# Taking the convolution's matmuls of layer 0 in steps inside its attention

## The chip, the cores and the metric

The kernel runs on one core of one Trainium2 chip. The metric is the device time of one execution in microseconds; before the change the median of three runs is 2084.97 us (2084.91 to 2086.41).

## The reference

Two blocks run on one sequence of 256 tokens of width 1024 (with 256 context tokens beside it in the first block). The change lies in layer 0 of the first block, cut here to what matters:

```python
def even_mixer(h_lat, h_ctx, w_in, conv_w, q_g, k_g, rpb, w_out, need_ctx):
    def query_side(p):
        gb, gc, u, q = jnp.split(p, [CONV_CH, 2 * CONV_CH, 3 * CONV_CH], -1)
        y_conv = gb * dwconv3(gc * u, conv_w)
        return y_conv, rms_norm(split_heads(q, NA_HEADS), q_g)
    ...
    p_lat = h_lat @ w_in
    ...
    y_na = merge_heads(neighbourhood_attention(q_lat, k_lat, v_lat, k_ctx, v_ctx, rpb))
    y_lat = jnp.concatenate([yc_lat, y_na], -1) @ w_out
```

The same is done for the context tokens (dense attention instead of the neighbourhood one). `gb`, `gc` and `u` are 512 columns each of one product with `w_in`; 8 heads of 64 attend over 512 keys (latent tokens) or 256 (context tokens). Beside it the layer's modulation vectors are products of silu(c), silu(c_ctx) with `ada_w`. A feed-forward stage, a second layer (two attentions, mixture of experts) and a second block follow.

## The kernel before

**Products.** Every fp32 product is made of three matmuls on high and low halves of both operands (`mm3`, L825 to L827: low x high, high x low, high x high). A weight tile (1 MB, 128 x 2048 in SBUF) is sent for by SyncE (`load_tiles`, L2741), its high half rounded by ScalarE (L1261), its low half subtracted by VectorE (L1754). Tiles stand in one list, `TILES`, in the order in which TensorE uses them (`use`). A tile gets the least recently used open slot; `t.prev` is the tile that had the slot before. SyncE sends for tiles strictly in list order, each when `t.prev` is done.

**Look-ahead.** ScalarE and VectorE call `feed(events)` ahead of each wait. `place[event]` is the number of tiles that TensorE's program has taken when it signals the event; with `n` the largest of these, `next_tiles` (L562) hands out tiles of the list, in order, up to `n + 2`, and stops at the first that may not be handed out:

```python
if t.gate != at["gate"] or t.slot not in at["slots"] or i >= n + at["sums" if t.sums else "ahead"] or (t.prev is not None and t.prev > n - 2):
    return
```

**Sum tiles.** A modulation product of 256 rows is done by VectorE alone (`summed`, L1760): four multiplications with a running sum (L1770) of raw tile and `CB`, the rows of silu(c), which ScalarE makes (L1420). Such tiles stand in the same list and slots (`sums`). For VectorE `at["sums"]` is 0 until layer 0's attention is over, so a sum tile i needs i < n; ScalarE (2) only passes over them. In the attention `pump(2)` does up to two of the four multiplications a step.

**Layer 0.** TensorE computes q, v and k (`proj`, two tiles each, four token tiles of 128), turning q by transpositions before k's product. The keys are normed by ScalarE (squares, L1385), VectorE (L1871, L1808, L1875) and GpSimd (L2640), turned (`head_turn`; VectorE L2059, ScalarE L1306, VectorE L1803). Then six convolution tiles (`feat`: c, u, g for channels 0 and 1, then for 2 and 3; two features of 128 channels a tile, 8 x 3 matmuls of 512 columns a feature), with the k transpositions behind the second tile. GpSimd masks the two bias tables (L2673) after the k norms. VectorE takes c x u, three taps, times g (L2093 to L2109).

**Attention** (`attend`, L908, L1308, L1960) runs 32 units, token tile by token tile, 8 heads each; the first 16 have 512 keys and a bias added by TensorE (L927), the other 16 have 256 keys. Step i gives TensorE: scores of unit i, transpositions (L831) of unit i-3, P·V (L948) of unit i-4, and after each token tile four more transpositions of its output. VectorE takes the maximum (L1978, L1984), ScalarE the exponential (L1318); they copy transposed probabilities in turns (L2009, L1326). Scores and transpositions share a ring of five PSUM banks. Twelve sum tiles (parts 2, 3, 4) stand at steps 1 + n*9//4, the gate rows of part 2 at step 16. The output projection (`proj` "o") follows.

Of the kernel before, what the change touches and what calls it, by code (L numbers as in the profile page):

```python
# [14 lines left out]
ALU = mybir.AluOpType  # L15
# [182 lines left out]
class Weight:  # L198
# [20 lines left out]

    def t(self):  # L220
        return Weight(self.name, None, self.at, True)
# [4 lines left out]
    def of(self, arrays):  # L226
        x = arrays[self.name][tuple(slice(*p) if isinstance(p, tuple) else p for p in self.at)]
        x = x.T if self.turned else x
        k, n = x.shape[0] // 128, x.shape[1]
        return x.reshape(k, 128, n).transpose(1, 0, 2).reshape(-1)  # L230


class Packed:
# [5 lines left out]
    def place(self, w):  # L239
        key = w.key()  # L240
        if key not in self.start:
            n = 1
            for p in w.at:
                n *= p[1] - p[0] if isinstance(p, tuple) else 1
# [23 lines left out]
def _build(nc, ctx, I, cst_d, scr_d, out_d, packed):  # L268
# [64 lines left out]
    XSa = Region("xs", LA.col).some(2, 1024)  # L333
    YC = v3(LA.pair(2048), 4)
# [7 lines left out]
    RP = CUB[:, 0:128]  # L342
    assert LA.col <= CB0
    XQ = [XSa[i // 2][:, (i % 2) * 512:(i % 2 + 1) * 512] for i in range(4)]
    slot_e = [slot(WORK + n) for n in (0, 4096, 14336, 18432, 22528)]
    LB = Region("att", LB0)
    YNT = v3(LB.pair(2048), 4)
    Pa = LB.some(4, 512)
    PTa = LB.some(2, 512)
    YNa = LB.some(2, 512)  # L350
    TMPa = LB.some(4, 512)
# [210 lines left out]
    def next_tiles(at, *events):  # L562
        n = max([place[event] for event in events], default=0)
        while at["tile"] < len(TILES):
            i, t = at["tile"], TILES[at["tile"]]
            if t.gate != at["gate"] or t.slot not in at["slots"] or i >= n + at["sums" if t.sums else "ahead"] or (t.prev is not None and t.prev > n - 2):
# [40 lines left out]
    class Heads:  # L607

        def __init__(self, units, lag, p, pt, fin):
            self.units, self.lag, self.p, self.pt, self.fin = units, lag, p, pt, fin  # L610
            self.slot_of, self.held, self.sums, self.gates = {}, {}, {}, {}
# [20 lines left out]
    HEADS = {}  # L632

# [89 lines left out]
    def mla_units():  # L723
# [13 lines left out]
        "a0": dict(fresh=[("clo", 3)], masks=[], out_free=[("clo", 3)]),  # L737
# [17 lines left out]
    CONV = ((512, "c"), (1024, "u"), (0, "g"))  # L755
# [3 lines left out]
    def tensor_program(e):  # L759
        due = Due(book)  # L760
        state = dict(tile=0, due=due, gate="", sums=iter(()))
# [21 lines left out]
        def sums(p, jj):  # L783
# [13 lines left out]
        def gate_rows(p):  # L797
            n = 8 * MODS[p][3]
            b = take("m", "gt", p)
# [4 lines left out]
        def consumed(t, *event):  # L804
            t.done = event
            for p, jj in itertools.islice(state["sums"], 1):
# [3 lines left out]
                 "m": (5,), "y": (4, 5, 6, 7)}  # L810
# [58 lines left out]

        def mod_product(p, hf, kh, ring="m"):  # L870
# [37 lines left out]
        def attend(st):  # L908
            A = HEADS[st]
            for i in A.steps():  # L910
                for p, jj in A.sums.get(i, ()):
                    sums(p, jj)
                if A.has(i):
# [3 lines left out]
                    for x, (q, keys) in enumerate(u.qk):  # L917
                        b = take("5", "score", st, i, x)
# [10 lines left out]
                        m.then_inc(*done("score", st, i, x))  # L929
                j = i - A.lag  # L930
                if A.has(j):
                    b = take("5", "turn", st, j)
# [19 lines left out]
                if A.has(j) and A.units[j].last:  # L952
                    g = A.units[j].group
                    y, nc_ = A.fin[g][:2]
                    b = take("5", "fin", st, g)
# [5 lines left out]
                if i in A.gates:  # L961
                    gate_rows(A.gates[i])
# [29 lines left out]
        for jj in range(2):  # L992
            for c0, nm in CONV:
                feat(("conv", nm, jj), AT4a, w_ev[:, c0:c0 + 512], 2 * jj, 2, 512, normed("a", 0) + normed("a", 1), "8")
                if jj == 0 and nm == "u":
                    for t in range(4):
                        head_turn(("k", t), XQ[t], 4, [("hn", "k", t)], "o")
        attend("a0")
# [10 lines left out]
        state["sums"] = iter([(p, jj) for p in (5, 6, 7, 8, 9, 10, 11) for jj in range(4)])  # L1009
# [239 lines left out]
    def scalar_program(e):  # L1249
# [58 lines left out]
        def attend(st):  # L1308
            A = HEADS[st]
            for i in A.steps():  # L1310
                if A.has(i):
# [1511 lines left out]
```

## Time and profile before

| | |
|---|---|
| median of three runs | 2084.97 us |
| the profiled execution, its span | 2084.66 us, 2082.8 us |
| PE busy | 1829.2 us (88%), 8622 matmuls |
| DVE, ACT, POOL busy | 1256.2, 819.2, 120.6 us |
| mean granted clock of TensorE | 0.874 of full |

PE is TensorE's matmuls, PEld its weight loads, DVE VectorE, ACT ScalarE, POOL GpSimd, SP SyncE. An idle time in brackets at a row's end stands before the instruction and names what ended it. A clock of 1.00 is 2.4 GHz, 0.50 is 1.2 GHz. Matmul ends are modelled, so the distance between starts is what to read.

### The profile page before, as it was taken

How to read it: one execution, taken by the hardware profiler on the slowest of the kernel's cores; microseconds unless marked ns; L12 is line 12 of the kernel's file. 1: busy time of each engine (PE TensorE's matmuls, PEld its weight loads, DVE VectorE, ACT ScalarE, POOL GpSimd, SP SyncE). 2: the span in 40 equal slices, each digit the busy share in tenths (PEclk: the TensorE clock that was granted, in tenths of full speed). 3: DMA queues.
4: the chain of work that ended last, by engine and by line, in shares of the span. 5: the costliest groups of instructions: out<-in, count | busy, mean ns of one | idle time of the engine just before them, and what ended most of it. 6: DMA issues, size and time to landing. Idle time of an engine off the chain costs nothing. (4 is left out here: it accounts for less than half of the span.)

```text
span 2082.8 us, 21348 instructions
## 1 busy us (share of the span) xinstructions
PE 1829.2 (88%) x8622; PEld 1526.9 (73%) x8622; DVE 1256.2 (60%) x1716; ACT 819.2 (39%) x993; POOL 120.6 (6%) x116
## 2 busy tenths in 40 slices
PE   4999997699999995969867999999968988878997
PEld 2787776578778884748646888888858866767986
DVE  5365674368665534544636988888866545555643
ACT  5322222322213314212314777777744432435532
POOL 1130000200020011220010000000000000000000
PEclk8899556799999997975676999999989985998999
DMA  6422241235555522210033888888844520125552
GB/s 277 118 91 91 81 142 61 81 130 194 213 197 188 195 77 72 101 61 21 1 146 112 324 327 324 329 323 330 330 176 162 194 97 1 61 82 193 182 201 101
DMA packets 61145, 332.54 MB, mean 160 GB/s; under 512 B 16803, under 2 KB 17378, under 8 KB 27889
## 3 DMA queue, kind: packets, MB, share of 16 engines
q1 hardware_dynamic: 55792, 321.54, 42.5%
q10 hardware_dynamic: 4354, 6.32, 1.0%
q0 software_dynamic: 896, 3.26, 0.4%
q8 instruction: 70, 1.15, 0.2%
q14 instruction: 33, 0.27, 0.0%
HBM read 329.96 MB, written 1.13 MB: 159 GB/s over the span
## 5 line engine op out<-in xcount | busy, mean ns | idle before, releaser
L1754 DVE TENSOR_TENSOR wlo__69<-raw__68,whi__70 128x2048 fp32r<-128x2048 f32 (+2 forms) x67 | 148.0, 2209 | 80.3 <-ACT whi__70 L1261 80.1
L1261 ACT ACTIVATE whi__70<-raw__68 128x2048 fp32r<-128x2048 f32 (+2 forms) x67 | 120.0, 1791 | 146.8 <-DMA raw__68<-in_ffn_w 69.6
L1754 DVE TENSOR_TENSOR wlo__61<-raw__60,whi__62 128x2048 fp32r<-128x2048 f32 (+4 forms) x54 | 121.1, 2243 | 92.2 <-ACT whi__62 L1261 92.2
L1754 DVE TENSOR_TENSOR wlo__65<-raw__64,whi__66 128x2048 fp32r<-128x2048 f32 (+4 forms) x54 | 104.0, 1927 | 55.9 <-ACT whi__66 L1261 55.8
L1261 ACT ACTIVATE whi__62<-raw__60 128x2048 fp32r<-128x2048 f32 (+4 forms) x54 | 98.1, 1816 | 82.6 <-DMA raw__60<-in_ev_w_in 30.5
L2640 POOL TENSOR_TENSOR keep__58<-keep__58,keep__59 128x1 f32<-128x1 f32 (+3 forms) x48 | 45.4, 946 | 1212.5 <-DVE keep__58 L1808 1212.5
L1261 ACT ACTIVATE whi__66<-raw__64 128x2048 fp32r<-128x2048 f32 (+4 forms) x54 | 87.4, 1619 | 62.0 <-DMA raw__64<-in_od_w_in 19.2
L1978 DVE TENSOR_REDUCE keep__58<-ps 128x1 f32<-128x256 f32 (+1 forms) x104 | 56.6, 544 | 40.9 <-PE ps L827 34.1
L1261 ACT ACTIVATE whi__145<-raw__143 128x2048 fp32r<-128x2048 f32 (+2 forms) x16 | 28.1, 1754 | 131.3 <-DMA raw__143<-in_ffn_w 131.3
L825 PE MATMUL ps<-ffn__124,wlo__144 128*128 128x512 f32 x176 | 69.8, 397 | 8.2 <-DVE wlo__144 L1754 7.0
L1754 DVE TENSOR_TENSOR wlo__144<-raw__143,whi__145 128x2048 fp32r<-128x2048 f32 (+2 forms) x16 | 33.5, 2091 | 64.7 <-ACT whi__145 L1261 64.7
L826 PE MATMUL ps<-ffn__125,whi__145 128*128 128x512 f32 x176 | 69.5, 395 | 0.0
L827 PE MATMUL ps<-ffn__124,whi__145 128*128 128x512 f32 x176 | 69.5, 395 | 0.0
L1770 DVE SCALAR_TENSOR_TENSOR wsum__67<-raw__64,silu_rows 128x1024 f32<-128x1024 f32 x56 | 68.6, 1252 | 0.5
L1770 DVE SCALAR_TENSOR_TENSOR wsum__63<-raw__60,silu_rows 128x1024 f32<-128x1024 f32 x56 | 68.6, 1252 | 0.5
L825 PE MATMUL ps<-ffn__124,wlo__69 128*128 128x512 f32 x168 | 66.1, 394 | 2.7 <-issue 2.7
L827 PE MATMUL ps<-ffn__124,whi__70 128*128 128x512 f32 x168 | 66.1, 394 | 0.0
L826 PE MATMUL ps<-ffn__125,whi__70 128*128 128x512 f32 x168 | 66.0, 393 | 0.0
L1754 DVE TENSOR_TENSOR wlo__222<-raw__221,whi__223 128x2048 fp32r<-128x2048 f32 x24 | 54.9, 2288 | 4.1 <-ACT whi__223 L1261 4.1
L1754 DVE TENSOR_TENSOR wlo__226<-raw__225,whi__227 128x2048 fp32r<-128x2048 f32 x24 | 54.9, 2288 | 0.0
L1754 DVE TENSOR_TENSOR wlo__230<-raw__229,whi__231 128x2048 fp32r<-128x2048 f32 (+1 forms) x24 | 50.7, 2112 | 3.8 <-ACT whi__231 L1261 3.8
L1261 ACT ACTIVATE whi__223<-raw__221 128x2048 fp32r<-128x2048 f32 x24 | 45.8, 1910 | 5.7 <-DMA raw__221<-in_moe_w 5.7
(1082 smaller groups left out, 5432.4 us busy)
## 6 DMA issues: line engine op xcount, KB each, us to landing
raw__221<-in_moe_w SPq DMA_DIRECT2D x24, 1024.0 KB, 6.2
raw__225<-in_moe_w SPq DMA_DIRECT2D x24, 1024.0 KB, 6.3
raw__60<-in_ada_w SPq DMA_DIRECT2D x19, 1024.0 KB, 6.9
raw__64<-in_ada_w SPq DMA_DIRECT2D x19, 1024.0 KB, 7.0
raw__229<-in_moe_w SPq DMA_DIRECT2D x16, 1024.0 KB, 5.7
raw__68<-in_moe_w SPq DMA_DIRECT2D x16, 1024.0 KB, 6.0
raw__60<-in_moe_w SPq DMA_DIRECT2D x16, 1024.0 KB, 6.8
raw__68<-in_ffn_w SPq DMA_DIRECT2D x14, 1024.0 KB, 4.9
```

Of the source, the lines that this page charges most:

```text
L825: e.matmul(out, ll, rh, start=start, stop=False)
L826: e.matmul(out, lh, rl, start=False, stop=False)
L827: return e.matmul(out, lh, rh, start=False, stop=stop)
L1261: e.activation(t.hi(), t.raw(), ACT.Copy).then_inc(*did("hi", i))
L1754: e.tensor_tensor(t.lo(), t.raw(), t.hi().bitcast(F32), ALU.subtract).then_inc(*did("lo", i))
L1770: m = e.scalar_tensor_tensor(out=junk, in0=slot_raw[t.slot][:, c * 1024:c * 1024 + 1024], scalar=1.0, in1=CB[:, v * D:(v + 1) * D], op0=AL ...
L1978: e.tensor_reduce(neg, b[:, 0:u.total], AX.X, ALU.max).then_inc(*link())
L2640: e.tensor_tensor(x, x, EXPO[:, 0:1].broadcast_to([128, n_]) if n_ > 1 else EXPO[:, 0:1], ALU.pow).then_inc(*did(out, *key))
```

## The change

The convolution's products are written as a generator, `convolved`, that yields after each step of three matmuls (96 steps, 8 a feature). Sixteen steps (features c0, u0) are taken before the first k transposition, the other 80 inside the attention, between the scores of unit i and the transpositions of unit i-3: `FILLED` gives 16 + (i+1)*80//28 steps taken after step i, so that step 27 takes the last. Features now go channel by channel (c, u, g), and a weight tile holds two features whose columns aren't adjacent (`Weight.columns`, laid side by side in the packed weights). VectorE's and ScalarE's parts of the convolution are called from `attend` one step after a feature is complete (`CONV_AT`), the final rounding of its output at steps 28 to 32.

Around it: the attention's ring has four banks, the convolution's two (4 and 5). Buffers move: the convolution's output `YC` takes the place of the normed input after it is last read, the probabilities lie in the q/k staging, the attention's output in the place of q. Two of the twelve sum tiles now stand in k's product, the other ten at steps 0, 3, ... 27; from k's product to the end of the attention, weight tiles use slots 0 and 1 and sum tiles slot 2. The gate rows come at step 12. silu(c) is made before k's squares. A sum's multiplications are taken one at each `feed`, or all when the tile after next is reached. `next_tiles` gets a stricter condition for the slot's last tile.

```diff
+        busy = max([i for i in range(max(n - 4, 0), n) if not TILES[i].sums], default=0)
         while at["tile"] < len(TILES):
             i, t = at["tile"], TILES[at["tile"]]
-            if t.gate != at["gate"] or ... or (t.prev is not None and t.prev > n - 2):
+            if t.gate != at["gate"] or ... or (t.prev is not None and t.prev >= min(n - 1, busy)):
                 return
...
-    for n, (p, jj) in enumerate((p, jj) for p in (2, 3, 4) for jj in range(4)):
-        HEADS["a0"].sums[1 + n * 9 // 4] = [(p, jj)]
-    HEADS["a0"].gates = {16: 2}
+    for n, (p, jj) in enumerate(SUMS[2:12]):
+        HEADS["a0"].sums[n * 3] = [(p, jj)]
+    HEADS["a0"].gates = {12: 2}
+    HEADS["a0"].ring = "4"
...
+    CONV = dict(c=512, u=1024, g=0)
+    FEATS = [(nm, j) for j in range(4) for nm in "cug"]
+    FILLED = [16 + (i + 1) * 80 // 28 if i < 27 else 96 for i in range(40)]
+    CONV_AT = {f: min(i for i in range(-1, 40) if ([16] + FILLED)[i + 1] >= 8 * (n + 1)) for n, f in enumerate(FEATS)}
...
-                s = min(open_slots, key=lambda s: last_in.get(s, s - 100))
+                s = min(state["loads"] or open_slots, key=lambda s: last_in.get(s, s - 100))
...
-                s = min(open_slots, key=lambda s: last_in.get(s, s - 100))
+                s = min(state["adds"] or open_slots, key=lambda s: last_in.get(s, s - 100))
...
+        def convolved():
+
+            w = W["ev_w_in"][0]
+            for f in range(0, 12, 2):
+                two = [(CONV[nm] + j * 128, CONV[nm] + j * 128 + 128) for nm, j in FEATS[f:f + 2]]
+                tile, hi, lo = use(w.columns(*two), KT, 256)
+                for i, key in enumerate(FEATS[f:f + 2]):
+                    b = take("c", "conv", *key)
+                    for k in range(KT):
...
+                        m = mm3(b, sub((hi, lo), slice(None), k, slice(i * 128, i * 128 + 128)),
+                                sub(AT4a, slice(None), k), k == 0, k == KT - 1)
...
+                        yield
...
                         m.then_inc(*done("score", st, i, x))
+                advance(fill, FILLED[i] - (FILLED[i - 1] if i else 16))
                 j = i - A.lag
...
+        state.update(sums=iter(SUMS[0:2]), loads=(0, 1), adds=(2,))
         proj(("l0", "k"), x4(AT4a), 4, KT, w_ev[:, 2048:2560], 512, rdy("a"))
...
+        state["sums"] = iter(())
+        for t in range(4):
+            if t == 0:
+                fill = convolved()
+                advance(fill, 16)
+            head_turn(("k", t), XQ[t], 4, [("hn", "k", t)], "o")
+        attend("a0", fill)
+        state.update(loads=None, adds=None)
```

VectorE's look-ahead and its part of the convolution:

```diff
         def feed(*events):
+            n = max([place[event] for event in events], default=0)
+            pump(9 if at["sum"] <= n - 2 else 1)
             for i, t in next_tiles(at, *events):
                 if t.sums:
                     pump(9)
-                    at["begun"] = summed(i, t)
-                    if at["sums"]:
+                    at["begun"], at["sum"] = summed(i, t), i
+                    if i <= n - 2:
                         pump(9)
                     continue
...
+        def convolved(i):
+            for j in range(4):
+                g, cv = GC[:, (j % 2) * 512:(j % 2 + 1) * 512], CV0[j]
+                if i == CONV_AT["u", j] + 1:
...
+                    feed(("prod", "conv", "u", j))
...
+                if i == CONV_AT["g", j] + 1:
+                    feed(("prod", "conv", "g", j))
...
+                if i == CONV_AT["g", 3] + 2 + j:
+                    feed(("prod", "conv", "g", 3))
+                    low("clo", (j,), YC[1][:, j, :], cv, YC[0][:, j, :], ("chi", j))
+        attend("a0", convolved)
         pump(9)
         at["sums"] = 2
```

## Rows read from the trace of the kernel before

**Rows 1.** Page, part 2: the clock granted to TensorE, 40 slices

```profile
PEclk8899556799999997975676999999989985998999
```

**Rows 2.** Windows: length, busy PE PEld DVE ACT POOL, clock, DMA share, GB/s

```profile
131.60:203.90 72.30, 68.99 (x305) 56.53 (x303) 41.41 (x44) 14.52 (x16) 16.82 (x6) 0.98 0.26 88
203.90:347.00 143.10, 124.26 (x484) 99.49 (x484) 96.67 (x195) 37.01 (x89) 1.14 (x2) 0.53 0.30 103
```

**Rows 3.** Windows, 10 us each, in the attentions a2 and a3

```profile
1720.00:1730.00 10.00, 10.00 (x34) 6.93 (x33) 4.69 (x15) 2.80 (x10) 0.00 (x0) 0.50 0.01 2
1800.00:1810.00 10.00, 9.21 (x61) 7.54 (x60) 5.67 (x20) 5.60 (x20) 0.00 (x0) 1.00 0.01 2
```

**Rows 4.** Timeline of PE, layer-0 attention: start, length, line, tiles, count

```profile
236.23 0.58 PE L825 MATMUL ps<-in__75,in__74 64*128 64x256 f32 x1
...
238.31 0.58 PE L825 MATMUL ps<-in__75,in__74 64*128 64x256 f32 x1
...
239.25 1.11 PE L831 MATMUL ps<-keep__49,att__113 128*128 128x128 f32 x4
240.16 1.81 PE L948 MATMUL ps<-in__77,att__116 128*128 128x64 f32 x8
241.89 0.58 PE L825 MATMUL ps<-in__75,in__74 64*128 64x256 f32 x1
```

**Rows 5.** Timeline of PE, the first steps of that attention

```profile
209.34 0.66 PE L831 MATMUL ps<-keep__49,att__112 128*128 128x128 f32 x4
209.93 0.38 PE L825 MATMUL ps<-in__75,in__74 64*128 64x256 f32 x1
...
211.10 0.38 PE L825 MATMUL ps<-in__75,in__74 64*128 64x256 f32 x1
...
211.65 0.66 PE L831 MATMUL ps<-keep__49,att__113 128*128 128x128 f32 x4
```

**Rows 6.** Timelines of SP and of ACT: weight tiles sent for and rounded

```profile
120.68 0.33 SPq L2741 DMA_DIRECT2D raw__64<-in_ev_w_in  x1
131.56 0.33 SPq L2741 DMA_DIRECT2D raw__68<-in_ev_w_in  x1
...
125.58 1.92 ACT L1261 ACTIVATE whi__66<-raw__64 128x2048 fp32r<-128x2048 f32 x1 [7.72 <-DMA raw__64<-in_ev_w_in]
```

**Rows 7.** Timeline of PE: last k transposes, start of output projection

```profile
158.14 0.66 PE L831 MATMUL ps<-keep__49,xs__79 128*128 128x128 f32 x4 [1.39 <-DVE xs__78 L2059]
158.55 0.56 PE L825 MATMUL ps<-in__84,wlo__69 128*128 128x512 f32 x1
...
162.28 0.39 PE L825 MATMUL ps<-in__84,wlo__69 128*128 128x512 f32 x1
...
346.27 0.78 PE L825 MATMUL ps<-whi__62,in__81 128*128 128x512 f32 x1
```

**Rows 8.** Timeline of DVE, from the q tiles to the convolution

```profile
116.08 0.69 DVE L1803 TENSOR_TENSOR in__74<-xs__79,in__73 128x512 fp32r<-128x512 f32 x1 [0.70 <-ACT in__73 L1306]
...
127.53 2.29 DVE L1754 TENSOR_TENSOR wlo__65<-raw__64,whi__66 128x2048 fp32r<-128x2048 f32 x1 [7.34 <-ACT whi__66 L1261]
129.74 0.68 DVE L1871 TENSOR_REDUCE keep__58<-in__86 128x8 f32<-128x512 f32 x1
...
142.69 6.07 DVE L1754 TENSOR_TENSOR wlo__69<-raw__68,whi__70 128x2048 fp32r<-128x2048 f32 x1
...
155.30 0.74 DVE L2059 TENSOR_SCALAR xs__78<-ps,keep__51 128x512 f32<-128x512 f32 x1
...
163.50 0.68 DVE L2093 TENSOR_TENSOR in__89<-in__88,ps 128x512 f32<-128x512 f32 x1
```

**Rows 9.** Timeline of POOL: the second bias table's mask

```profile
146.57 6.65 POOL L2673 TENSOR_TENSOR in__83<-in__83,keep__49 128x2048 f32<-128x2048 f32 x1
```

**Rows 10.** Timeline of DVE: two of a sum tile's four multiplications

```profile
207.83 1.23 DVE L1770 SCALAR_TENSOR_TENSOR wsum__63<-raw__60,silu_rows 128x1024 f32<-128x1024 f32 x1
...
208.98 1.22 DVE L1770 SCALAR_TENSOR_TENSOR wsum__63<-raw__60,silu_rows 128x1024 f32<-128x1024 f32 x1
```

More of the change, by code:

```diff
@@ L226, in of @@
     def of(self, arrays):
-        x = arrays[self.name][tuple(slice(*p) if isinstance(p, tuple) else p for p in self.at)]
+        x = arrays[self.name]
+        if isinstance(self.at[-1][0], tuple):
+            x = np.concatenate([x[..., slice(*span)] for span in self.at[-1]], -1)
+        at = [p for p in self.at if not (isinstance(p, tuple) and isinstance(p[0], tuple))]
+        x = x[tuple(slice(*p) if isinstance(p, tuple) else p for p in at)]
         x = x.T if self.turned else x
@@ L342, in _build @@
     RP = CUB[:, 0:128]
+    PTa = LA.some(2, 512)
     assert LA.col <= CB0
@@ L345, in _build @@
     slot_e = [slot(WORK + n) for n in (0, 4096, 14336, 18432, 22528)]
+    YNT, Pa = QT3, XQ
+    YNa = [BREV[0][:, t * 512:(t + 1) * 512] for t in range(2)]
     LB = Region("att", LB0)
[L347 to L351, printed above, removed]
+    YC, TMPa = v3(LB.pair(2048), 4), LB.some(4, 512)
     LF = Region("ffn", WORK)
@@ L563, in next_tiles @@
         n = max([place[event] for event in events], default=0)
+        busy = max([i for i in range(max(n - 4, 0), n) if not TILES[i].sums], default=0)
         while at["tile"] < len(TILES):
             i, t = at["tile"], TILES[at["tile"]]
-            if t.gate != at["gate"] or t.slot not in at["slots"] or i >= n + at["sums" if t.sums else "ahead"] or (t.prev is not None and t.prev > n - 2):
+            if t.gate != at["gate"] or t.slot not in at["slots"] or i >= n + at["sums" if t.sums else "ahead"] or (t.prev is not None and t.prev >= min(n - 1, busy)):
                 return
@@ L632, in _build @@
     HEADS = {}
+    SUMS = [(p, jj) for p in range(2, 12) for jj in range(4)]
     def prob(st, i):
@@ L760, in tensor_program @@
         due = Due(book)
-        state = dict(tile=0, due=due, gate="", sums=iter(()))
+        state = dict(tile=0, due=due, gate="", sums=iter(()), loads=None, adds=None)
         open_slots, turn_of = [0, 1, 2] + slot_e, Counter()
@@ L795, in sums, with gate_rows @@
                 last_in[s] = i
-        def gate_rows(p):
+        def gate_rows(p, ring="m"):
             n = 8 * MODS[p][3]
-            b = take("m", "gt", p)
+            b = take(ring, "gt", p)
             for s, n_ in state["due"](("gsum", p)):
@@ L917, in attend @@
                     for x, (q, keys) in enumerate(u.qk):
-                        b = take("5", "score", st, i, x)
+                        b = take(A.ring, "score", st, i, x)
                         at = 0
@@ L954, in attend @@
                     y, nc_ = A.fin[g][:2]
-                    b = take("5", "fin", st, g)
+                    b = take(A.ring, "fin", st, g)
                     for s, n in state["due"](("fy", st, g)):
@@ L1008, in tensor_program @@
             lent[slot_f] = [("prod", "o", 0, 1, 3), ("res", ("o", 0), 1, 3)]
-        state["sums"] = iter([(p, jj) for p in (5, 6, 7, 8, 9, 10, 11) for jj in range(4)])
+        state["sums"] = iter(SUMS[12:])
         nf = normed("f", 0) + normed("f", 1)
@@ L1731, in vector_program @@
     def vector_program(e):
-        at = dict(tile=0, due=Due(book), gate="", chain=0, ahead=2, sums=0, slots={0, 1, 2, *slot_e}, begun=None)
+        at = dict(tile=0, due=Due(book), gate="", chain=0, ahead=2, sums=0, slots={0, 1, 2, *slot_e}, begun=None, sum=0)
         def due(*events):
```

140 lines of the change are left out of this document (67 added, 73 removed).

## The prediction

> **What bounds the kernel now.** I read the page's clock line first, then the stages, then single steps. TensorE is the busiest engine, and its clock is granted at about half for three slices, 220 to 350 us [rows 1]. The windows say what that is: from 131.6 to 203.9 us the convolution's products run at 0.98, from 203.9 to 347 the attention of layer 0 runs at 0.53 with TensorE busy for 124 of 143 us [rows 2]. It is not the dependence on softmax that sets this stage but TensorE at 1.2 GHz; VectorE is busy for 96.7 us of it. The clock is no fixed property of attention: the later attention a2 stood at 0.50 while never idle, a3 at 1.00 with gaps in it [rows 3].
>
> One wide step (units 0 to 15) at half clock repeats every 5.66 us (236.23 to 241.89): scores 3.02, transpositions 0.91, the P·V products 1.73; one block of 256 keys is 0.94 of it [rows 4]. At 2.4 GHz the same pieces took 1.72 (209.93 to 211.65), 0.59 and 0.55 for the block [rows 5]. No P·V of this stage ran at full clock, so I take half of 1.73, 0.87 (an estimate). A step of the convolution is three matmuls of 512 columns. A tile of 48 of them is 10.9 us at full clock (120.68 to 131.56, when SP could reuse its slot) [rows 6], 0.227 each, 0.68 a step. After the short waits of the k turns nine of them took 3.73 (158.55 to 162.28), 0.41 each, 1.24 a step, until the clock was back: 1.7 us lost [rows 7]. The output projection starts at 346.3 [rows 7]. VectorE writes a tile's low half in 2.29 us; the k norms take 13.0 (129.74 to 142.7), the k turns 8.2 (155.30 to 163.50); between them two low halves took 12.6 instead of 5.3 [rows 8], while POOL masked the bias tables, until 153.2 [rows 9].
>
> **The change, step by step.** The work of TensorE stays: 96 convolution steps, 32 units. 16 steps now stand ahead of the k transpositions and 80 go 2 to 3 at a time between score i and transposition i-3. If nothing waited and the clock stayed up, the interleaved stage would cost 16 x (1.72+0.59+0.87) = 50.9, 16 light units x (0.55+0.30+0.44) = 20.6, four output turns 2.4, and 80 x 0.68 = 54.4: 128.3 us [rows 5, 6]. That is the gain. Against it stand waits that come from the order in which halves are prepared. The low half of a tile is written by VectorE in list order, a sum tile (a modulation product) can't begin before TensorE's program has passed it, and what lies behind it in the list waits too.
>
> *k's second tile.* A sum tile now stands ahead of it in the list. VectorE is free at 116.8 [rows 8], but its rows of silu(c) are computed on ScalarE only after the last q rounding, about 1.9 us like a copy of the same size [rows 6]: 118.0. Four multiplications 1.15 apart [rows 10] end at 122.7, the low half at 125.0. TensorE wants it at 120.7, where tile one was given back [rows 6]. 4.3 us idle, 1.7 for the clock: k ends at 137.6, not 131.6.
>
> *The first convolution tile.* Its transfer stands on SP's queue behind that of the second sum tile, which waits for the first sum (122.7). One load takes 4.9 us [rows 6]; I take 7.8 for the second of two (an estimate, 7 to 9). ScalarE waits for it ahead of k's squares, rounds until 132.4, squares until 133.0; the norms end 13.0 later, at 146.0. Then come the second sum, 4.6, and the low half, 2.3: 152.9. The bias masks start on POOL at the same point of its program as before, so I add the 7.3 us that the collision cost [rows 8, 9]: 160.2 (bounds 152.9 and 160.2; I take the upper since the two subtracts were hit alike). TensorE stands for 22.6 us. The 16 steps, 10.9 + 1.7, end at 172.8. The k turns' chain, 0.6 + 8.2, has no products beneath it any more: scores begin at 181.6, 22 us ahead of before, with 80 steps still to do.
>
> By the Trainium skill (SBUF — State Buffer, Who interferes with whom) a VectorE instruction with two SBUF inputs contends with a GpSimd instruction that reads SBUF, so the sum's multiplications should be slowed like the subtracts. By that rule the 160.2 stands; were sums exempt, it would be 156.5. The rows show only the subtracts.
>
> *Start of the attention.* VectorE first does the first channel's taps (four operations of 0.5 to 0.75, 2.7) and a low half (2.3), against 3.0 of scores: 2 us. The clock is down after the wait: 3. ScalarE's look-ahead holds an exponential while a sum is finished: 1. Together 6.
>
> *Three waits inside.* The sum tiles at steps 9, 15 and 21 reuse slot 2 straight after another sum tile. The new condition in the look-ahead lets such a tile through only for an event counted after a later product tile; that product tile, the next of the convolution, stands behind it. So at steps 11, 17 and 22 TensorE asks for a tile whose halves VectorE writes only after this step's maximum (0.85 wide, 0.6 narrow), the whole sum (4.6) and its subtract (2.3): 7.8 less one convolution step 0.7 is 7.1; 7.5; and 7.5 less 1.4 plus about 2 for a late transfer, 8. Behind the waiting matmul are queued the step's transpositions and P·V. 22.6 us in all. A stand of this length before had the clock down, so each costs half-clock time besides: 1.7 as in that row's stretch [rows 7] if the products were dense, up to 6 as they are mixed; I take 3, 9 in all.
>
> *The end.* The draining steps have nothing beneath them: 4. The last sum tile (step 27) is let through only after the attention, ahead of the output projection's first low half: final rounding and subtract 1.7, 4.6, 2.3 = 8.6. Before, that half lay ready.
>
> *At nothing:* the ring of four PSUM banks (a score needs the exponential of two steps before, 0.85 + 0.9 us against steps of 5.1; if that cover goes it is one of the waits above); the two convolution banks (given back one feature, 2.8 steps, earlier); moved buffers; gate rows at step 12 on PE, VectorE and POOL, needed over 100 us later; VectorE's load, at most 96.7 + 41.4 us [rows 2] in 179. Sums in the feed-forward stage are begun in one look-ahead and finished in the next: same work, 0, bounds -4 and +4.
>
> **Sum:** 181.6 + 128.3 + 6 + 22.6 + 9 + 4 + 8.6 = 360.1 us for the output projection's start, against 346.3: +13.8. The profiled execution took 2084.66 us (span 2082.8), 0.3 below the median of 2084.97: 2098.5 from the one, 2098.8 from the other; I say 2098. The bounds of the steps (collision 0, clock 1.7 to 6 each, transfer, feed-forward) give this case 2084 to 2118.
>
> **The rivals.**
> *The halves come in time inside the attention* (faster). Place: steps 11, 17, 22 and the projection's start. If the sum is done early there, 22.6 + 9 + 6.9 = 38.5 go: 2060. It decides from 14 us on, so gaining little more than a third of it is enough. If the two waits ahead of the attention go as well (4.3 + 1.7 + 22.6 + 1.7 = 30.3), 2030. For it: VectorE has some 40 us of slack in the stage, and transfers are early. Against it: the order is a static list, and slack can't be used by what isn't let through.
>
> *The clock stays at half* (much slower). At 1.2 GHz the stage is 16 x 5.66 + 16 x 2.26 + 3.6 = 130.4 [rows 4] plus 80 x 1.24 = 99.2 [rows 7]: 229.6 instead of 128.3, less the 12 already allowed: +89, 2187; each tenth of the stage at half clock is 10 us. For it: 80 us of that attention never lifted it, and every long wait drops it. Against it: the clock came back within 3.9 us of 512-column products [rows 7], and a3 kept 1.00 with small matmuls.
>
> The Trainium skill (Perfetto Trace Analysis, Matmul Optimizations) says that the matmul engine scales its power with utilization and that matmuls should be executed back to back in batches, which speaks against cutting twelve batches into pieces. By that rule the time is this rival's; the trace shows the clock going either way in attentions [rows 3].
>
> **How the numbers follow.** Forecast 0.50; halves in time 0.28; in between (some of the waits, 2075 to 2089) 0.10; clock at half for much of the stage 0.12. Within 0.2% (4 us, about what a measurement of this kernel can tell from no change) lie most of the in-between case and the forecast's edge: 0.10. Faster 0.31, slower 0.59. The range leaves out the full rival of 2030 (0.07) and most of the half-clock case (0.09): 2052 to 2130. The likeliest case's own range is 2084 to 2118.
>
> **What would show it.** TensorE's first convolution matmul near 160 us, waiting for VectorE; three waits of 6 to 9 us of a first-term matmul (now in the convolution) for a low half, each behind four sum multiplications; one of 7 to 9 at the output projection; clock near 1.00 between them. Wrong if low halves of convolution tiles are written before the sum preceding them or more than a step ahead of use, if the clock reads 0.5 through the interleaved steps, or if the feed-forward stage moves by over 4 us.

## The result and the profile after

The changed kernel is slower: 2119.76 us (median of four executions, 2112.61 to 2128.69) against 2084.94 (2083.86 to 2086.41), a ratio of 1.0169, 95% interval 1.0122 to 1.0215. The forecast was 2098, range 2052 to 2130: right in direction and inside the range, 22 us short, and just outside the likeliest case's own range (2084 to 2118). The profiled execution took 2125.05 us (span 2123.2, mean clock 0.880), 5.3 above its median. The four times stand in two pairs, 2112.61 and 2114.46, 2125.05 and 2128.69, with the median between them where no execution lies; the profiled one is of the slower pair. That matters below.

The page of the kernel after: busy tenths of TensorE and granted clock in 40 slices of 53 us, to hold against [rows 1].

```profile
PE   4958887869899996887975999999986989787997
PEclk8976897979999998895675999999998985898999
```

The slices of half clock of before (5, 5, 6) are gone. From the fourth to the eighth slice stand 6 to 9, and TensorE's busy time has fallen to 1813.5 us of 2123.2, from 1829.2 of 2082.8: much of its time at half clock was exchanged for time in which it stands. Where it stands, from k's second tile to the output projection (rows of PE: start, duration, line and operation, and in brackets the idle time before it and what ended it; in this kernel L839 is the first matmul of a triple, L845 a transposition):

```profile
124.76 0.77 PE L839 MATMUL ps<-whi__62,in__87 128*128 128x512 f32 x1 [4.46 <-DVE wlo__61 L1797]
160.26 0.76 PE L839 MATMUL ps<-in__86,wlo__65 128*128 128x512 f32 x1 [21.53 <-issue]
...
182.48 0.55 PE L839 MATMUL ps<-in__75,in__74 64*128 64x256 f32 x1 [4.88 <-ACT in__75 L1346]
187.38 0.76 PE L839 MATMUL ps<-in__86,wlo__61 128*128 128x512 f32 x1 [1.83 <-issue]
258.60 0.77 PE L839 MATMUL ps<-in__86,wlo__61 128*128 128x512 f32 x1 [7.02 <-issue]
298.44 0.77 PE L839 MATMUL ps<-in__86,wlo__65 128*128 128x512 f32 x1 [8.79 <-issue]
326.95 0.77 PE L839 MATMUL ps<-in__86,wlo__61 128*128 128x512 f32 x1 [6.77 <-issue]
...
374.83 0.76 PE L839 MATMUL ps<-whi__66,att__115 128*128 128x512 f32 x1 [8.83 <-DVE wlo__65 L1797]
```

These are the waits of the prediction, one by one: k's second tile (forecast 4.3, at 125.0), the first convolution tile (forecast at 160.2), the scores (181.6), three inside the attention (7.1, 7.5, 8: 22.6; measured 22.58), the projection (8.6). In five of the rows the bracket says only "issue"; the row's second operand, `wlo`, is a low half, and VectorE's rows ahead of the matmul at 258.60 show who wrote it and after what:

```profile
250.72 0.69 DVE L2025 TENSOR_REDUCE keep__58<-ps 128x1 f32<-128x512 f32 x1 [4.39 <-PE ps L841]
251.44 0.15 DVE L2031 TENSOR_SCALAR keep__58<-keep__58 128x1 f32<-128x1 f32 x1
251.51 1.22 DVE L1813 SCALAR_TENSOR_TENSOR wsum__71<-raw__68,silu_rows 128x1024 f32<-128x1024 f32 x1
...
255.07 1.22 DVE L1813 SCALAR_TENSOR_TENSOR wsum__71<-raw__68,silu_rows 128x1024 f32<-128x1024 f32 x1
...
256.21 2.29 DVE L1797 TENSOR_TENSOR wlo__61<-raw__60,whi__62 128x2048 fp32r<-128x2048 f32 x1
```

The maximum, four multiplications of the sum, the subtract. Just ahead VectorE had stood for 4.39 us: it had the time, but the list didn't let it have the tile. ScalarE is held by the same list: the tile was sent for at 237.30, and its high half was rounded only from 252.31.

The balance of the two profiled executions (spans 2082.8 and 2123.2, +40.4), from the starts of the same events: output projection's first matmul 346.27 and 374.83, +28.6 (forecast +13.8); last gating behind the projection 391.82 and 421.07, +0.7 more; last gating of the feed-forward stage 792.83 and 829.20, +7.1 more (forecast 0, bounds -4 and +4; a second profile of the same kernel, after_again below, gives +5.1); first gating behind the second layer's attention 1065.76 and 1105.31, +3.2 more; the rest +0.9.

### The profile page after: what moved, and what is told of

Same layout as the page of the kernel before. It is cut to its first block and busy times, and to the rows that moved or that the text cites. A ratio compares the mean times of both kernels' runs of the same rounds, so it can differ in the third digit from the quotient of the medians.

```text
span 2123.2 us, 21351 instructions
## 1 busy us (share of the span) xinstructions
PE 1813.5 (85%) x8622; PEld 1508.2 (71%) x8622; DVE 1255.3 (59%) x1716; ACT 819.4 (39%) x993; POOL 122.2 (6%) x116
## 5 line engine op out<-in xcount | busy, mean ns | idle before, releaser
L1797 DVE TENSOR_TENSOR wlo__69<-raw__68,whi__70 128x2048 fp32r<-128x2048 f32 (+3 forms) x64 | 136.2, 2129 | 71.9 <-ACT whi__70 L1301 71.9
L1301 ACT ACTIVATE whi__70<-raw__68 128x2048 fp32r<-128x2048 f32 (+3 forms) x64 | 114.2, 1785 | 141.0 <-DMA raw__68<-in_ffn_w 66.4
L1301 ACT ACTIVATE whi__62<-raw__60 128x2048 fp32r<-128x2048 f32 (+4 forms) x56 | 91.3, 1630 | 102.8 <-DMA raw__60<-in_ev_w_in 47.7
L1301 ACT ACTIVATE whi__66<-raw__64 128x2048 fp32r<-128x2048 f32 (+4 forms) x55 | 100.0, 1817 | 67.4 <-DMA raw__64<-in_ev_w_in 21.8
L1301 ACT ACTIVATE whi__141<-raw__139 128x2048 fp32r<-128x2048 f32 (+2 forms) x16 | 28.1, 1754 | 141.6 <-DMA raw__139<-in_ffn_w 141.6
L1797 DVE TENSOR_TENSOR wlo__140<-raw__139,whi__141 128x2048 fp32r<-128x2048 f32 (+2 forms) x16 | 33.5, 2092 | 79.4 <-ACT whi__141 L1301 79.4
L839 PE MATMUL ps<-ffn__120,wlo__140 128*128 128x512 f32 x176 | 69.9, 397 | 8.3 <-DVE wlo__140 L1797 7.2
L839 PE MATMUL ps<-ffn__120,wlo__69 128*128 128x512 f32 x168 | 65.5, 390 | 2.7 <-issue 2.7
L1813 DVE SCALAR_TENSOR_TENSOR wsum__71<-raw__68,silu_rows 128x1024 f32<-128x1024 f32 x48 | 65.3, 1385 | 2.2 <-ACT silu_rows L1445 1.2
L1813 DVE SCALAR_TENSOR_TENSOR wsum__67<-raw__64,silu_rows 128x1024 f32<-128x1024 f32 x40 | 50.4, 1283 | 0.5
L1813 DVE SCALAR_TENSOR_TENSOR wsum__63<-raw__60,silu_rows 128x1024 f32<-128x1024 f32 x40 | 49.4, 1257 | 0.5
```

Source lines behind the costliest of these rows:

```text
L839: e.matmul(out, ll, rh, start=start, stop=False)
L1301: e.activation(t.hi(), t.raw(), ACT.Copy).then_inc(*did("hi", i))
L1797: e.tensor_tensor(t.lo(), t.raw(), t.hi().bitcast(F32), ALU.subtract).then_inc(*did("lo", i))
L1813: m = e.scalar_tensor_tensor(out=junk, in0=slot_raw[t.slot][:, c * 1024:c * 1024 + 1024], scalar=1.0, in1=CB[:, v * D:(v + 1) * D], op0=AL ...
```

## Experiments

The theory: each wait comes from the order in which tiles are let through, at the place where the prediction put it; the clock's loss behind the waits adds to it. The rivals: the clock is held down by the mixture of matmuls itself, or VectorE has no slack. Times of the kernel before, measured beside each group: 2083.14 us (13 executions) beside the first four runs, 2083.87 (7) beside the best three, 2082.91 (7) beside `first_step` and `after_again`, 2082.33 (13) beside the last. All code below is cut; "..." marks what is left out.

### two_slots: two buffers for the sums

```diff
...
+        if book.counting:
+            last_in.update({s: last_in[2] for s in slot_h})
+            state["adds"] = slot_h
         attend("a0", fill)
...
```

> Inside the attention the sum tiles get two raw buffers (the two halves of slot 2) in turn, so that no sum tile reuses the buffer of the tile just before it and none is held back by the look-ahead; nothing else is changed. Theory A (the waits come from the order in which halves are let through, and the clock falls because of them): the three waits of 7.0, 8.8 and 6.8 us at a convolution matmul and the 8.8 us at the output projection go, 31.4 us, and with them up to 8 us of half clock between 250 and 370 us. The projection starts at 335 to 344 instead of 374.8 and the time is 2080 to 2089 instead of 2119.8. Theory B (the mixed stage itself holds the clock down): the waits go, but the clock reads 0.5 to 0.8 in their place, projection not before 355, time 2100 or more. Theory C (VectorE has no slack): the waits come back as waits of scores for the maxima, time 2110 or more.

Measured: 2092.39 us (10 executions, 2085.12 to 2101.03), 1.0053 of before [1.0035, 1.0071]; 27 us less than the changed kernel's 2119.76, 3 us above what theory A gave. (The two buffers are the halves of slot 2; the products' unused output goes to one idle buffer, so each multiplication also waits for the one before it.) All three waits inside and the one at the projection are gone from the rows, and the projection starts at 349.99 instead of 374.83. But 24.8 us came, not 31 to 40: other waits took part of their place. Its rows of PE with more than 1.5 us of idle time between 190 and 350 us:

```profile
294.09 1.71 PE L997 MATMUL ps<-in__77,in__93 128*128 128x64 f32 x8 [3.29 <-ACT in__93 L1384]
...
335.33 1.12 PE L997 MATMUL ps<-in__77,in__93 128*128 128x64 f32 x4 [4.50 <-ACT in__93 L1384]
...
349.99 0.76 PE L850 MATMUL ps<-whi__66,att__118 128*128 128x512 f32 x1 [1.56 <-issue]
```

P·V (L997) waits for ScalarE's copy of the transposed probabilities. At 294 ScalarE had been held in its look-ahead by a late transfer, with an exponential and that copy queued behind:

```profile
291.19 1.91 ACT L1317 ACTIVATE whi__62<-raw__60 128x2048 fp32r<-128x2048 f32 x1 [7.72 <-DMA raw__60<-in_ev_w_in]
```

That transfer was sent for at 282.74, behind a sum's on SP's queue (282.37), which had to wait for its buffer until the sum before it was done. At 335 it was VectorE, with two multiplications and the closing product of a convolution channel (330.79 to 333.80) ahead of a maximum in the light steps. So theory A holds for the waits; B doesn't from 220 to 290 us, where the clock reads 1.00; C holds for one wait of 4.5 us. What this run leaves as it was is the half clock at the attention's start: 0.50 until 212 us here too.

### late_sums: and no sum in k's product

```diff
...
-    for n, (p, jj) in enumerate(SUMS[2:12]):
-        HEADS["a0"].sums[n * 3] = [(p, jj)]
-    HEADS["a0"].gates = {12: 2}
+    for i, (p, jj) in zip((1, 3, 6, 9, 12, 15, 18, 20, 23, 25), SUMS[0:10]):
+        HEADS["a0"].sums[i] = [(p, jj)]
+    HEADS["a0"].gates = {14: 2}
...
-        state.update(sums=iter(SUMS[0:2]), loads=(0, 1), adds=(2,))
+        state.update(loads=(0, 1))
...
+        state.update(loads=None, adds=None, sums=iter(SUMS[10:12]))
...
```

> The same two buffers, and no sum tile in k's product: ten sums stand at steps 1 to 25 of the attention, never more than two between two convolution tiles, the last two in the output projection. Theory A: k's second tile is not waited for (4.5 us), the first convolution matmul starts near 133 us instead of 160.3, the scores at 155 to 160 instead of 182.5, and the clock, which read 0.50 from 180 to 210 us after the long wait, is back within some 5 us: projection start 300 to 315, time 2045 to 2062. Theory B (the half clock at the attention's start belongs to the mixed stage and not to the wait before it): again 25 to 30 us at 0.50 behind the first scores, time 2060 to 2075. Theory C: VectorE, with more in fewer us, makes the scores wait; time 2075 or more.

Measured: 2065.31 us (4 executions, 2058.97 to 2069.06), 0.9916 [0.9886, 0.9945]: 3 us above theory A's range and within B's in time, with its projection at 310.89 as A had it. The clock tells the two apart. Its rows of PE at the k turns, the first scores and the projection:

```profile
149.22 1.12 PE L856 MATMUL ps<-keep__49,in__79 128*128 128x128 f32 x4 [4.23 <-DVE in__78 L2122]
154.12 1.12 PE L856 MATMUL ps<-keep__49,in__79 128*128 128x128 f32 x4 [3.79 <-DVE in__78 L2122]
159.66 0.55 PE L850 MATMUL ps<-in__75,in__74 64*128 64x256 f32 x1 [4.42 <-ACT in__75 L1362]
...
310.89 0.76 PE L850 MATMUL ps<-whi__66,att__118 128*128 128x512 f32 x1 [1.56 <-issue]
```

The clock was back some 5.9 us behind the first scores (0.50 until 165 us, 1.00 from 166), not 25 to 30 as B had it, and it read 1.00 from 170 to 280: with the same steps mixed in, the stage holds full clock for 110 us on end. What differs from the changed kernel is the waits.

### ffn_finish: the feed-forward stage's old rule

```diff
-                    if i <= n - 2:
+                    if at["sums"] or i <= n - 2:
                         pump(9)
```

> Only the rule of the feed-forward stage is put back: a sum begun there is finished in the same look-ahead. If this rule made the new wait of 4.7 us at 579.6 us and the rest of the 7 us by which the stage became longer, the distance from the output projection's last gating to the last one of the feed-forward stage falls from 408 to about 401 us and the time by 7 us, to 2113. If the stage is longer for another reason (tiles that arrive later, the clock), nothing moves.

Measured: 2112.49 us (2110.05, 2114.93). Two executions say nothing of a gain, as five of the changed kernel's eight (below) are about as fast; the distance within the profile does. From the projection's last gating to the stage's last: 400.7 us (417.70 to 818.42), 408.1 in the changed kernel (406.1 in after_again), 401.0 before. All of the 5 to 7 us are this line's. How it works, in the changed kernel (PE's wait, the subtract it waited for, and SP's two issues before it; L2786 sends for a tile):

```profile
579.55 0.77 PE L839 MATMUL ps<-whi__141,ffn__128 128*128 128x512 f32 x1 [4.66 <-DVE wlo__140 L1797]
...
577.12 2.29 DVE L1797 TENSOR_TENSOR wlo__140<-raw__139,whi__141 128x2048 fp32r<-128x2048 f32 x1 [3.46 <-ACT whi__141 L1301]
...
567.85 0.33 SPq L2786 DMA_DIRECT2D raw__64<-in_ada_w  x1
568.22 0.43 SPq L2786 DMA_DIRECT2D raw__139<-in_ffn_w  x1
```

and in ffn_finish, the same two transfers and the same matmul:

```profile
558.04 0.43 SPq L2786 DMA_DIRECT2D raw__64<-in_ada_w  x1
563.11 0.33 SPq L2786 DMA_DIRECT2D raw__139<-in_ffn_w  x1
...
572.91 0.47 PE L839 MATMUL ps<-whi__141,ffn__128 128*128 128x512 f32 x1 [1.36 <-DVE wlo__140 L1797]
```

The two kernels stand 3.3 us apart here (the product tile sent for before these, into raw 139, at 550.10 and 546.79); the rest of each distance is the edit's. A sum begun in one look-ahead and finished in the next moves the moment at which its slot (raw 64) is free: it is sent for at 567.85 instead of 558.04, 6.5 us later beyond the 3.3. SP sends in list order, so the product tile behind it (raw 139) starts 1.8 us late, and it now travels beside the sum's tile: ScalarE has it 6.95 us after its sending (568.22 to 575.17) instead of 5.13 (563.11 to 568.24). Both together make the wait longer, 4.66 us instead of 1.36. I had put the spreading at "same work, 0"; the work was the same, the moment at which the buffer came free was not.

One more thing is seen here by accident. Ahead of the feed-forward stage this is the changed kernel, and yet its projection starts at 371.36, not at 374.83; first_step and after_again below take this up.

### masks_early: the bias masks ahead of the k norms

```diff
...
         for w in ("q", "k"):
+            if w == "k":
+                for t in range(2):
...
+                    for s, n in due(("brev",), ("cst",), ("lo", place["prod", "l0", "k", 3] - 1)):
...
```

> GpSimd masks the bias tables ahead of the k norms (once k's second low half is written, about 125 us) instead of behind them. If the collision made the second sum cost 12.8 instead of 4.6 us, its four multiplications take about 1.2 us each, the k norms end some 1.5 us later because GpSimd is busy until 135, and the first convolution matmul starts at 153 to 154.5 instead of 160.3; time 2112 to 2115. If the multiplications were slow for another reason they stay at 4.9 and 5.5 us and the start at 160 to 162.

Measured: 2111.99 us (2109.52, 2114.47; again two, hardly below the changed kernel's faster five, so the rows decide), first convolution matmul at 152.98 (expected 153 to 154.5) instead of 160.26. The second sum of the changed kernel, while GpSimd masked (144.52 to 154.45):

```profile
145.20 4.90 DVE L1813 SCALAR_TENSOR_TENSOR wsum__71<-raw__68,silu_rows 128x1024 f32<-128x1024 f32 x1
...
150.03 5.50 DVE L1813 SCALAR_TENSOR_TENSOR wsum__71<-raw__68,silu_rows 128x1024 f32<-128x1024 f32 x1
...
155.57 1.22 DVE L1813 SCALAR_TENSOR_TENSOR wsum__71<-raw__68,silu_rows 128x1024 f32<-128x1024 f32 x1
```

and of this kernel, with GpSimd masking from 124.65 to 133.78:

```profile
145.90 1.22 DVE L1813 SCALAR_TENSOR_TENSOR wsum__71<-raw__68,silu_rows 128x1024 f32<-128x1024 f32 x1
```

So a multiplication with two SBUF inputs took four times as long beside GpSimd's addition; the two together were 8.0 us longer, and the first convolution matmul moved by 7.3. The Trainium skill (SBUF — State Buffer, Who interferes with whom) says that a VectorE instruction with two SBUF inputs contends with a GpSimd instruction that reads SBUF, which the prediction had weighed; the trace agrees, 4.90 and 5.50 against 1.22 us.

### best: all three edits together

> late_sums with both other edits: sums of the feed-forward stage finished where they are begun, and the bias masks made on GpSimd as soon as VectorE has written the last turned q. Theory A (the losses are single waits with places of their own, and add): the k turns lose the waits of 4.2, 3.8 and 4.4 us at 149 to 160 us, which stand over low halves and turns slowed by the masks, so the scores start at 151 to 154 instead of 159.7 (-7), and the feed-forward stage gives 6 to 7: 2065.3 - 13 to 14 = 2051, range 2046 to 2056. Theory B (the parts share one slack): only the feed-forward part shows, 2058 to 2060.

Its masks wait for `("qlo", "q", 3)` instead. Measured: 2055.28 us (4 executions, 2054.45 to 2056.20), 0.9864 [0.9848, 0.9881]: faster than before by 28.6 us. The feed-forward stage gave its 6.4 (400.25 us against 406.67 in late_sums). The masks gave 3.1, not 7: scores start at 156.58. Rows of PE and, last, of DVE:

```profile
124.07 0.47 PE L850 MATMUL ps<-whi__62,in__87 128*128 128x512 f32 x1 [3.20 <-DVE wlo__61 L1813]
...
156.58 0.55 PE L850 MATMUL ps<-in__75,in__74 64*128 64x256 f32 x1 [4.88 <-ACT in__75 L1362]
...
310.33 0.76 PE L850 MATMUL ps<-whi__66,att__118 128*128 128x512 f32 x1 [1.56 <-issue]
...
119.92 4.00 DVE L1813 TENSOR_TENSOR wlo__61<-raw__60,whi__62 128x2048 fp32r<-128x2048 f32 x1 [2.92 <-ACT whi__62 L1317]
```

The collision moved onto another subtract: the one for k's second tile takes 4.00 us where it took 2.29, and TensorE waits 3.20 us for it, 1.49 in late_sums. And of the three waits that the expectation put down to the masks the last didn't go: 4.88 us ahead of the scores, as in the changed kernel.

### best_chunk: a whole feature at a time

```diff
...
-    FILLED = [16 + (i + 1) * 80 // 28 if i < 27 else 96 for i in range(40)]
+    FILLED = [16 + (i + 1) * 10 // 28 * 8 if i < 27 else 96 for i in range(40)]
...
```

(and the last sum inside at step 26 instead of 25)

> As best, but the convolution is taken a whole feature (8 steps, 24 matmuls of 512 columns, some 5.5 us) at a time, ten times in the attention, instead of 2 or 3 steps in every unit. If what holds the clock at half in the first steps of the attention is that its matmuls are mixed with small ones, the longer runs of large ones bring it back earlier: the stage up to 5 us shorter, 2043 to 2051. If short waits decide it, the clock's course is that of best; but transpositions and P·V stand behind 5.5 us of convolution and seven steps of ten have none, so maxima are waited for in the light steps: 2053 to 2065.

Measured: 2064.63 us (4 executions, 2064.24 to 2065.22), 9.3 more than best. The clock was back 12 us behind the first scores (0.82 in 167 to 169 us), later than in best (6 us, 0.83 in 162 to 164), and new waits stand behind softmax: 2.00 at 178.57, 4.03 at 269.70, 3.67 at 308.57. Long batches between softmax steps bought nothing here. The Trainium skill (Perfetto Trace Analysis, Matmul Optimizations) says that the matmul engine scales its power with utilization and wants its matmuls back to back in batches, which the prediction made a rival of. The runs agree only in part: these batches of 24 are slower than the finer mixture, but best_block, next, takes 48 on end and has the clock back soonest of all.

### best_block: sixteen steps in one run ahead of the scores

```diff
...
-    FILLED = [16 + (i + 1) * 80 // 28 if i < 27 else 96 for i in range(40)]
+    FILLED = [32 + (i + 1) * 64 // 28 if i < 27 else 96 for i in range(40)]
...
+        advance(fill, 16)
...
         attend("a0", fill)
...
```

(sums at steps 0, 1, 4, 8, 11, 15, 18, 22, 25, three in the projection)

> As best, but 16 more convolution steps are taken in one run between the k turns and the first scores, and 64 instead of 80 in the attention. After the waits of the k turns the kernel before had the clock back within 3.9 us of 512-column products. Theory clock: it is back within 4 to 6 us here, the scores start 11 us later than in best with the clock at 1.00 and stay there; the stage is as long as in best or up to 4 us shorter, 2047 to 2052. Theory cover: 64 steps cover less of the light steps, where VectorE is the bound; the waits behind them grow by 2 to 8 us, 2053 to 2059.

Measured: 2050.62 us (4 executions, 2049.44 to 2053.71), 0.9842 [0.9826, 0.9858], the fastest. The clock was back 3 us behind the first matmul after the k turns (156.53; 0.63 in 158 to 160, 1.00 from 160), and the projection started at 307.51, 2.8 us ahead of best. The cover that it gave up cost little: the longest wait of the stage is 3.21 us (186.66), and in the light steps 1.37.

### first_step and after_again: where 16 us of spread come from

```diff
-        HEADS["a0"].sums[n * 3] = [(p, jj)]
+        HEADS["a0"].sums[n * 3 or 1] = [(p, jj)]
```

> The changed kernel with one edit: the first sum tile of the attention stands at step 1, behind the second convolution tile, instead of at step 0 ahead of it. So this tile's low half is written before the attention and the wait of 1.83 us at 187.4 us, 5 us behind the first scores, goes. In late_sums and best, without such a second wait, the clock was back 5 to 6 us behind the first scores; in the changed kernel 30 us behind them (in ffn_finish and masks_early, the same program there, 13). Theory: the second short wait is what leaves the clock down so long and makes it differ between executions. Then it reads 1.00 from about 189 us, the projection starts 6 to 15 us earlier, the time is 2105 to 2113 and its spread of 16 us shrinks to a few. Rival: it comes back at one of several moments whatever the first step does; then a gain of 1 to 3 us from the wait alone (or a loss of that much, as the low half moves into the k turns) and the same spread.

> The changed kernel once more, for the clock's course between 182 and 215 us and for the spread of its time beside first_step. If the clock's return differs between executions of one program, this profile shows 1.00 from about 196 or from about 212 us, with scores at 182.5 in both, and the times lie between 2110 and 2129.

after_again, the changed kernel itself: 2114.40 us (2112.02, 2112.48, 2116.32, 2125.74). With the first four that makes eight executions: five between 2112.0 and 2116.3, three between 2125.0 and 2128.7, with a median of 2115.4. Windows of TensorE from the first scores on (stretch, its length, busy time and matmuls, then the granted clock); the changed kernel's profile of above:

```profile
182.00:188.00 6.00, 3.69 (x10) 0.50 0.00 0
188.00:196.00 8.00, 8.00 (x21) 0.50 0.26 90
196.00:212.00 16.00, 16.00 (x41) 0.50 0.20 86
212.00:250.00 38.00, 38.00 (x208) 0.99 0.23 84
```

after_again, scores at 183.30:

```profile
188.00:196.00 8.00, 7.80 (x19) 0.50 0.16 41
196.00:212.00 16.00, 16.00 (x77) 0.97 0.27 112
```

One program, the same waits, and the clock is back at some 196.8 or 212.7; in 16 us 77 or 41 matmuls are done. The first inside wait ends at 252.03 instead of 258.60. two_slots shows 212, ffn_finish 196, and masks_early 13 us behind its scores too. So ffn_finish's projection started 3.5 us earlier; not 8, because its clock took 13 us behind the first inside wait (251.17) and not 5.

first_step: 2120.61 us (2119.41 to 2122.62). The short wait at 187.4 is gone, and the clock is back 6 to 7 us behind the first scores:

```profile
182.00:189.00 7.00, 6.36 (x16) 0.50 0.00 0
189.00:208.00 19.00, 19.00 (x92) 1.00 0.30 111
```

The spread is 3.2 us. So a late and uncertain return went along with the second short wait, 1.83 us with 3 us of work between it and the 4.88 ahead of the scores: 13 or 30 us in the five profiles that have it, 6 us in first_step, late_sums and best, which don't. That the pair is the cause is not shown. best_chunk has no second wait and took 12 us, a single wait inside the attention took 13 us in ffn_finish and masks_early, and of the 18 executions of the changed kernel and two_slots 11 are in the faster group (to 2116.3 and to 2093.0), so four of four there by luck would be no rarity (0.14, an estimate from these counts). But the gain in time didn't come, because I had missed what the edit does to the list:

```profile
216.34 0.76 PE L839 MATMUL ps<-in__86,wlo__65 128*128 128x512 f32 x1 [6.53 <-issue]
```

With the sum at step 1 behind the second convolution tile, it stands right ahead of the next sum, at step 3: a fourth pair of neighbours in slot 2, and at step 5, where the third convolution tile is due, a fourth wait of 6.5 us. An expectation missed, and with two_slots the clearest evidence for the mechanism: a wait of 6.5 us or more inside the attention appears where two sum tiles stand side by side in one slot, and only there.

### before_masks: the kernel before with the masks moved

> The kernel before with one edit: GpSimd masks the bias tables when the last turned q is written, as in best. It tells how much of best's gain over the kernel before comes from the interleaving and how much from this move. If the interleaving carries it: the k turns lose at most their waits of 1.9 and 1.4 us and the half clock behind them (1.7), and k's product may wait a little for a low half written during the masks, so 2079 to 2084. If the move carries it: 2060 or less.

Measured: 2081.09 us (10 executions, 2079.82 to 2082.58), 0.9994 [0.9985, 1.0004]: no difference that counts. The gain of best over the kernel before lies in the interleaving and the placing of the sums, which no run tells apart.

## Why the prediction came out as it did

**k's second tile, the first convolution tile, the scores:** 124.76, 160.26 and 182.48 against 125.0, 160.2 and 181.6. The steps through VectorE's queue held, the collision too (7.3 taken; masks_early moves the start by 7.3).

**The three waits:** 7.02, 8.79, 6.77 against 7.1, 7.5, 8; the middle one had a sum's closing addition and a channel's taps in it besides. two_slots, which takes the neighbours out of one slot, and first_step, which adds a pair, show that they are the cause.

**The clock behind the three waits:** back 5, 3 and 9 us behind them, half of which is lost: 8.5 us in all, 9 taken. In ffn_finish the first of them cost 13 us at half, so this sum, too, is not fixed.

**The clock at the start of the attention: the term that was mis-sized.** I took 3 us; the nearest row had dense 512-column matmuls, with the clock back in 3.9 us [rows 7], and here they are mixed with small ones. It read 0.50 from the scores at 182.5 to 212.7 in the profiled execution, 30 us, of which half, 15, is lost, 30 again in two_slots, and 13 us in the three others with these steps. The failing step is to price the clock's return by one value from one row; the second short wait, 3 us of work behind the first, was costed as standing and no more. Why it took 30 us in some executions and 13 in others stays open. This is 12 of the 14.7 us by which the projection came later than forecast (374.8 and 360.1); 0.9 was there at the scores, and some 2 lie in the drain and in small gaps that I have not split.

**The projection's wait:** 8.83 against 8.6.

**The feed-forward stage: the term left out.** +7.1 us (+5.1 in after_again), where I had 0 with bounds of 4 and had named a move of over 4 us as a sign of being wrong. That sign came. I had costed the multiplications and not the slot's release, though the prediction used just that chain (sum, slot, SP, transfer) ahead of the attention.

**Still open:** 3 us in the second layer (from the feed-forward stage's last gating to the first one behind the attention 276.1 us against 272.9). Every kernel here with the changed list shows 1.7 to 3.6 of them; no run was made on it.

**How much the hit is worth.** The places and sizes of the waits were right. The rest missed to one side: in the profiled execution 14.7 us at the projection's start, 7 in the feed-forward stage and some 5 elsewhere. The likeliest case's own range ended at 2118; that the median of 2119.76 still counts as inside is owed to the margin above it, which took in the mild end of the half-clock case. The faster five of the eight executions, 2112 to 2116, lie within both.

**What held the clock down before.** I wrote that the stage was set by the clock and not by the dependence on softmax, and put the half clock at 220 to 350 us. The windows have it from 213 to 349, and what stands at its start is a wait for softmax, the only one above 0.5 us until 304. PE's row in the kernel before:

```profile
217.36 1.94 PE L948 MATMUL ps<-in__77,att__116 128*128 128x64 f32 x8 [5.05 <-DVE att__116 L2009]
```

From 222 to 304 us TensorE was busy for 81.64 of 82 us, with the attention's small matmuls alone, and the clock stayed at 0.50. With the convolution's matmuls among them it came back behind every wait. So not the waits alone decide: they lower the clock, and what TensorE is fed behind them goes along with how soon it is back.

**The rivals.** The clock at half for the whole stage is refuted: the changed kernel's profile reads 1.00 for some 109 of the 192 us between first scores and projection, late_sums for 110 us on end. The halves in time (2060, or 2030 with both waits ahead of the attention gone as well) are what late_sums and best make of the kernel: 2065 and 2055. They stay above 2030 because of transfers that hold ScalarE (best: 2.89 us at 256.30), a drain at 0.50 and the second layer's 3 us.

## What to carry to other kernels

Where an in-order look-ahead hands out tiles of two kinds, look at the list for neighbours that share a buffer: behind each such pair stands a full preparation in the open, however idle the engine was just before. Spreading work over more calls costs nothing in work and still moves the moment at which its buffer comes free, and with an in-order queue every transfer behind it. And a filler of large matmuls in a stage of small ones that runs at half clock pays (28.6 and 33.3 us of 2083 here), once its operands are ready a step ahead. Where the clock's return varies between executions, one profile is not enough to price it.

## What the hardware showed

In layer 0's attention with the convolution mixed in, the granted clock came back 3 to 13 us behind a single long wait of TensorE inside it (3 behind 298.44 in the changed kernel, 13 behind 251.17 in ffn_finish), and 13 or 30 us behind the first of two waits close together, different between executions of one program (30 in the changed kernel's first profile and in two_slots, 13 in after_again, ffn_finish and masks_early). Without the convolution, in the kernel before, it stayed at 0.50 for some 132 us behind a wait of 5.05 us, the last 45 of them with further waits. The times: 16.7 us of spread in the changed kernel's eight executions and 15.9 in two_slots' ten, against 3.2 in first_step and 1.8 in best, with four each; the kernel before has 2.5 in four executions and 9.2 in thirteen, so a small spread of four is weak evidence. late_sums, with three waits of 4 us up to its scores, spread by 10.1, and why is open. A multiplication of two SBUF operands on VectorE took 4.90 to 5.50 us beside GpSimd instead of 1.22, a subtract 4.00 instead of 2.29. Of two 1 MB transfers sent for 0.4 us apart in best the second was ready for ScalarE only 8.0 us after its sending (245.39 to 253.39), against 4.9 for one alone [rows 6].
